# The first stage of a conv / mLSTM / MLA kernel: weights and input loaded by turns, two slabs in whole precision

## The chip, the cores and the metric

One core of a Trainium2 chip runs the whole program. The metric is the device time of one execution in microseconds. The kernel before took 2867.58 us (median of three runs, 2866.63 to 2867.74).

## The reference, cut to what matters

Two layers over 1024 latent and 256 context tokens of width 1024. Layer 0 mixes by a short convolution and an mLSTM, layer 1 by latent attention. Each layer begins with a modulation of its input, and only that of layer 0 is touched here:

```
sh_l, sc_l, g_l = split(silu(c) @ mod_w[0] + mod_b[0], 3)      # latent tokens
sh_c, sc_c, g_c = split(silu(c_ctx) @ mod_w[0] + mod_b[0], 3)  # context tokens
u_lat = x * (1 + sc_l) + sh_l
u_ctx = ctx * (1 + sc_c) + sh_c
gates = u @ ev_w_in[:, G0:G0+16]                               # 16 gate columns, in the same stage
```

All arithmetic is float32 in the reference.

## The kernel before, in words

`stage_modulate` is the first of the kernel's stages. It makes u transposed (features on the partitions, 1280 tokens along the rows) as a pair of tiles, `u_hi` and `u_lo`, whose sum is the float32 value: a high half in TensorE's rounded format (fp32r) and the rest. All large products of the kernel take three matmuls of such halves (`mm3`, L38 to L42: high x high, low x high, high x low).

The 1024 features go in eight blocks of 128, k = 0 to 7. A beat handles one block:

- A slab of `mod_w` is needed: columns 128k to 128k+127 of the shift and of the scale, for all 1024 input features, 8 x 256 float32 values on each partition. Slabs 0 and 1 are loaded alone, 2 and 3, 4 and 5, 6 and 7 as pairs (`load_slab`, L147). ScalarE copies a slab into its high half (`w_high`, L222), VectorE subtracts (`w_low`, L258).
- TensorE sums silu(c) times the slab into 4 rows (`row_sums`, L323): the four columns of `cs` (the high and low half of the two vectors) are the stationary side, and for each of the 8 blocks of input features the slab's high and low half move past, 16 matmuls of 256 columns. ScalarE copies the 4 rows out (L209).
- TensorE transposes the ten 128x128 tiles of the input (`turn`, L342), in three token chunks: j = 0 with 256 tokens (the context), j = 1 and 2 with 512 each, in the order 1, 2, 0.
- TensorE turns the 4 rows into columns with the matrix `sel` (`columns`, L332, the selection), and VectorE adds the bias (L267): now the scale and shift of block k stand one on each partition.
- ScalarE and VectorE evacuate the transposed tiles with that scale and shift: ScalarE writes `u_hi` for all three chunks (`high`) and the float32 value for chunk 2 (`whole`), VectorE the float32 value for chunks 0 and 1. Then VectorE subtracts for chunk 2 (`low`, L282), GpSimd for chunks 1 and 0 (L194).
- TensorE multiplies u by the gate weights (`gates`, L356), nine matmuls a block, two beats later.

The order on each engine is written out by hand, in one loop over k for each engine, with semaphores between them. TensorE: row sums of k, gates of k-2, transposes of k, selection of k; the gates of the last three blocks follow the loop. VectorE: column add, evacuations, `w_low(k + 2)`, `low(k, 2)`. ScalarE: `u(k)`, with the rows of k+1 copied inside it, then `w_high(k + 3)`.

All loads of the stage are issued by SyncE on one queue: c, ident, slab 0, `sel`, the bias, the input's block 0, slab 1, the gate weights, slabs 2 and 3, input blocks 1 and 2, slabs 4 and 5, input blocks 3 and 4, slabs 6 and 7, input blocks 5 to 7 (`SPANS`, L76), the gate bias, and the first weights of the next stage (L182), which ScalarE and VectorE also split here (L255, L318). The stage ends with a barrier of all engines.

Of the kernel before, what the change touches and what calls it, by code (L numbers as in the profile page):

```python
# [9 lines left out]
P = 128  # L10
KD = D // P
# [16 lines left out]
ALU = mybir.AluOpType  # L28
# [3 lines left out]
def f(ap):  # L32

    return ap.bitcast(F32)
# [39 lines left out]
def stage_modulate(nc, a, keep):  # L74

    SPANS = ((0, 1), (1, 3), (3, 5), (5, 8))  # L76
    PAIR_AT = (0, 1, 2, 0)
    u_hi, u_lo, mod_col, ident = keep["u_hi"], keep["u_lo"], keep["mod_col"], keep["ident"]
# [9 lines left out]
    with ExitStack() as ctx:  # L88
# [12 lines left out]
        cs = s.sb("cs", [P, KD, 4], F32R)  # L101
        sel = s.sb("sel", [4, 2])
# [6 lines left out]
        x_in = [[s.sem(f"x_in{q}{j}") for j in range(3)] for q in range(4)]  # L109
# [6 lines left out]
        u_hi_ok, u_raw_a, u_raw_d, u_lo_d, u_lo_p = (s.sem(n) for n in ("u_hi_ok", "u_raw_a", "u_raw_d", "u_lo_d", "u_lo_p"))  # L116
        gw_zero, gw_hi_ok, gw_ok, first_hi = (s.sem(n) for n in ("gw_zero", "gw_hi_ok", "gw_ok", "first_hi"))
# [24 lines left out]
        arrival = lambda k: k if k < 2 else 1 + k // 2  # L142

        @block.sync
        def _(sp):
# [51 lines left out]
        def _(act):  # L197
# [15 lines left out]
            def u(k):  # L213
                act.wait_ge(col_ok, k + 1)
                high(k, 1)
                high(k, 2)
                whole(k, 2)
                if 0 < k < KD - 1:
                    row_sums(k + 1)
                high(k, 0)  # L220

            def w_high(k):  # L222
                if k == 0:
                    for half in range(2):
                        act.wait_ge(w0_in[half], 16)
                        nc.scalar.copy(high_of(0)[:, :, half, :], slab(w_raw, 0)[:, :, half, :]).then_inc(w_hi_ok, 1)
                    return
                act.wait_ge(w_in[arrival(k)], 32)
                if k >= 2:
                    act.wait_ge(r_done, k - 1)  # L230
                nc.scalar.copy(high_of(k), slab(w_raw, k)).then_inc(w_hi_ok, 1)
# [5 lines left out]
            w_high(0)  # L237
            row_sums(0)
            w_high(1)
# [18 lines left out]
        def _(dve):  # L258
            def w_low(k):
                for half in range(2) if k == 0 else ():  # L260
                    dve.wait_ge(w_hi_ok, half + 1)
                    nc.vector.tensor_tensor(slab(w_lo, 0)[:, :, half, :], slab(w_raw, 0)[:, :, half, :], f(high_of(0)[:, :, half, :]), ALU.subtract).then_inc(w_lo_ok, 1)
                if k:
                    dve.wait_ge(w_hi_ok, k + 2)
                    nc.vector.tensor_tensor(slab(w_lo, k), slab(w_raw, k), f(high_of(k)), ALU.subtract).then_inc(w_lo_ok, 1)
# [16 lines left out]
            def low(k, j):  # L282
# [4 lines left out]
            nc.vector.memset(ones[:, :], 1.0).then_inc(ones_ok, 1)  # L287
            dve.wait_ge(c_t, 1)
# [3 lines left out]
                                    0.5, None, ALU.mult).then_inc(c_ok, 1)  # L292
            dve.wait_ge(cs_hi, 1)
            dve.wait_ge(c_ok, 1)
            nc.vector.tensor_tensor(cs[:, :, 2:4], c_silu[:, :, :], f(cs[:, :, 0:2]), ALU.subtract).then_inc(cs_ok, 1)
            w_low(0)
# [3 lines left out]
            for k in range(KD):  # L300
                columns(k)
                whole(k, 0)
                whole(k, 1)
                if k == 0:
                    w_low(1)
                    low(0, 2)
# [5 lines left out]
                else:  # L312
                    if k + 2 < KD:
                        w_low(k + 2)
                    low(k, 2)
                if k == KD - 2:
                    dve.wait_ge(first_hi, 1)
                    nc.vector.tensor_tensor(wv_lo[:, :, :], w_first[:, :, :], f(wv_hi[:, :, :]), ALU.subtract)  # L318

        @block.tensor  # L320
        def _(pe):
            def row_sums(k):
                pe.wait_ge(w_lo_ok, k + 2)  # L323
# [3 lines left out]
                for kk in range(KD):  # L327
                    nc.tensor.matmul(sums, cs[:, kk, :], high_of(k)[:, kk, :, :], start=kk == 0, stop=False)
                    last = nc.tensor.matmul(sums, cs[:, kk, :], slab(w_lo, k)[:, kk, :, :], start=False, stop=kk == KD - 1)
# [2289 lines left out]
```

## Time and profile before

| | us |
|---|---|
| median of the runs | 2867.58 |
| the profiled execution, its own time | 2864.85 |
| its span | 2863.1 |
| TensorE busy | 2829.3 (99%) |
| VectorE busy | 1543.3 (54%) |
| ScalarE busy | 1185.2 (41%) |
| GpSimd busy | 285.7 (10%) |

The page cuts the span into 40 slices of 71.6 us; the first slice is about the stage of this case:

```
PE   7999999999999999999999999999999999999998
PEld 5888888888888888888887888888888888888886
DVE  6646554555366536654353325666666666666544
ACT  6323322332233223342243315666666666666500
```

Each digit is the busy share of a slice in tenths. In the rows, PE is TensorE's matmuls, PEld its weight loads, DVE VectorE, ACT ScalarE, POOL GpSimd, SP SyncE. The granted clock is given as a share of 2.4 GHz, so 0.50 is 1.2 GHz.

### The profile page before, as it was taken

How to read it: one execution, taken by the hardware profiler on the slowest of the kernel's cores; microseconds unless marked ns; L12 is line 12 of the kernel's file. 1: busy time of each engine (PE TensorE's matmuls, PEld its weight loads, DVE VectorE, ACT ScalarE, POOL GpSimd, SP SyncE). 2: the span in 40 equal slices, each digit the busy share in tenths (PEclk: the TensorE clock that was granted, in tenths of full speed). 3: DMA queues.
4: the chain of work that ended last, by engine and by line, in shares of the span. 5: the costliest groups of instructions: out<-in, count | busy, mean ns of one | idle time of the engine just before them, and what ended most of it. 6: DMA issues, size and time to landing. Idle time of an engine off the chain costs nothing. (4 is left out here: it accounts for less than half of the span.)

```text
span 2863.1 us, 38077 instructions
## 1 busy us (share of the span) xinstructions
PE 2829.3 (99%) x15377; PEld 2430.1 (85%) x15377; DVE 1543.3 (54%) x2793; ACT 1185.2 (41%) x1979; POOL 285.7 (10%) x298
## 2 busy tenths in 40 slices
PE   7999999999999999999999999999999999999998
PEld 5888888888888888888887888888888888888886
DVE  6646554555366536654353325666666666666544
ACT  6323322332233223342243315666666666666500
POOL 5100000000000000001232001202202022020000
PEclk9999999999999999999999999999999999999999
DMA  7311130113111311163361320010000100002332
GB/s 211 100 34 47 47 122 26 53 49 114 32 47 47 116 39 48 45 217 103 111 196 51 126 81 34 27 35 23 28 26 27 38 20 32 26 24 103 126 102 75
DMA packets 221504, 200.76 MB, mean 70 GB/s; under 512 B 12085, under 2 KB 193221, under 8 KB 221330
## 3 DMA queue, kind: packets, MB, share of 16 engines
q1 hardware_dynamic: 208578, 184.91, 20.9%
q0 software_dynamic: 2352, 8.17, 0.8%
q10 hardware_dynamic: 10400, 5.24, 0.6%
q8 instruction: 123, 2.02, 0.3%
q14 instruction: 51, 0.42, 0.0%
HBM read 157.34 MB, written 40.95 MB: 69 GB/s over the span
## 5 line engine op out<-in xcount | busy, mean ns | idle before, releaser
L40 PE MATMUL e_pj<-e_u_hi,e_w_hi 128*128 128x512 f32 (+1 forms) x864 | 307.9, 356 | 1.0 <-PEq L58 1.0
L40 PE MATMUL e_pj<-e_u_hi,v_w_hi 128*128 128x512 f32 (+1 forms) x864 | 307.7, 356 | 0.2 <-DVE v_kk_lo L882 0.2
L41 PE MATMUL e_pj<-e_u_lo,e_w_hi 128*128 128x512 f32 (+1 forms) x864 | 306.0, 354 | 0.0
L41 PE MATMUL e_pj<-e_u_lo,v_w_hi 128*128 128x512 f32 (+1 forms) x864 | 306.0, 354 | 0.0
L42 PE MATMUL e_pj<-e_u_hi,v_w_lo 128*128 128x512 f32 (+1 forms) x864 | 305.8, 354 | 0.0
L42 PE MATMUL e_pj<-e_u_hi,e_w_lo 128*128 128x512 f32 (+1 forms) x864 | 305.7, 354 | 0.0
L2241 ACT CAST t_pt_hi<-t_ring 128x512 fp32r<-128x512 f32 (+1 forms) x384 | 181.4, 519 | 232.3 <-PE t_ring L2447 232.3
L2330 DVE TENSOR_TENSOR t_pt_lo<-t_ring,t_pt_hi 128x512 fp32r<-128x512 f32 (+1 forms) x384 | 216.0, 597 | 52.6 <-ACT t_pt_hi L2241 50.9
L2257 ACT ACTIVATE t_prob<-t_scores,t_bias 128x1280 f32<-128x1280 f32 x128 | 170.6, 1333 | 87.7 <-DVE t_bias L2351 87.5
L42 PEld LDWEIGHTS e_pj<-e_u_hi,v_w_lo 128*128 128x128 f32 x864 | 163.2, 189 | 23.2
L42 PEld LDWEIGHTS e_pj<-e_u_hi,e_w_lo 128*128 128x128 f32 x864 | 163.1, 189 | 23.1
L40 PEld LDWEIGHTS e_pj<-e_u_hi,v_w_hi 128*128 128x128 f32 x864 | 163.3, 189 | 22.4 <-issue 0.9
L40 PEld LDWEIGHTS e_pj<-e_u_hi,e_w_hi 128*128 128x128 f32 x864 | 163.2, 189 | 22.1 <-issue 1.2
L41 PEld LDWEIGHTS e_pj<-e_u_lo,v_w_hi 128*128 128x128 f32 x864 | 163.4, 189 | 20.7
L41 PEld LDWEIGHTS e_pj<-e_u_lo,e_w_hi 128*128 128x128 f32 x864 | 163.2, 189 | 20.4
L2262 ACT ACTIVATE t_prob<-t_prob,t_rec 128x1280 f32<-128x1280 f32 x128 | 177.0, 1382 | 7.4 <-DVE t_rec L2355 7.4
L2447 PEld LDWEIGHTS t_ring<-k_ident,t_prob 128*128 128x128 f32 x1280 | 147.2, 140 | 16.7
L2447 PE MATMUL t_ring<-k_ident,t_prob 128*128 128x128 f32 x1280 | 160.3, 272 | 0.0
L656 POOL TENSOR_TENSOR v_wgt<-v_wgt,v_mask 128x128 f32<-128x128 f32 x80 | 41.3, 519 | 1039.2 <-DMA v_wgt<-r_rows 1039.0
L40 PE MATMUL t_scores<-t_kn_hi,t_qn_hi 128*128 128x256 f32 x381 | 140.3, 368 | 2.0 <-ACT t_prob L2257 2.0
L41 PE MATMUL t_scores<-t_kn_lo,t_qn_hi 128*128 128x256 f32 x381 | 135.6, 356 | 0.0
L2500 PE MATMUL t_scores<-l_kr_lo,t_qs 128*128 128x256 f32 x381 | 135.6, 356 | 0.0
(500 smaller groups left out, 6700.2 us busy)
## 6 DMA issues: line engine op xcount, KB each, us to landing
e_w_raw<-in_ev_w_in SPq DMA_DIRECT2D x72, 512.0 KB, 4.7
v_mw<-in_mod_w SPq DMA_DIRECT2D x32, 512.0 KB, 3.7
l_w_raw<-in_od_w_in SPq DMA_DIRECT2D x21, 512.0 KB, 3.9
o_m_raw<-mixT SPq DMA_DIRECT2D x20, 512.0 KB, 5.4
o_w_raw<-in_ev_w_out SPq DMA_DIRECT2D x16, 512.0 KB, 8.8
zgT<-l_lat_q SPq DMA_DIRECT2D x16, 512.0 KB, 3.8
t_zg<-zgT SPq DMA_DIRECT2D x32, 256.0 KB, 2.8
ogT<-t_zg SPq DMA_DIRECT2D x32, 256.0 KB, 2.0
```

What stands on the lines that cost most here:

```text
L40: nc.tensor.matmul(out, whi, xhi, start=first, stop=False)
L41: nc.tensor.matmul(out, whi, xlo, start=False, stop=False)
L42: return nc.tensor.matmul(out, wlo, xhi, start=False, stop=last)
L656: pool.tensor_tensor(wgt[d][x][:, :], wgt[d][x][:, :], mask[:, d, :], ALU.add).then_inc(masked, 1)
L2241: nc.scalar.copy(dst, src).then_inc(ring_hi, 1)
L2257: nc.scalar.activation(prob[x][:, :], S[:, 0:T], ACT.Exp, bias=bias[x][:, :], accum_out=total[x][:, :]).then_inc(exp_ok, 1)
L2262: nc.scalar.mul(prob[x][:, :], prob[x][:, :], rec[x][:, :]).then_inc(prob_ok, 1)
L2330: nc.vector.tensor_tensor(dst, src, hi, ALU.subtract).then_inc(ring_free, frees(op))
L2447: last = nc.tensor.transpose(ps[:, c * P:(c + 1) * P], prob[t % 2][:, (c0 + c) * P:(c0 + c + 1) * P], ident[:, :])
L2500: last = nc.tensor.matmul(out, qs[b][:, tok], kr2[1][:, k0:k0 + n], start=False, stop=True)
```

## The change: what it does

- The input is loaded in five spans (0), (1), (2, 3), (4, 5), (6, 7), and the loads go by turns: input 0, slab 1, input 1, the gate weights, then for each pair its slabs and its input blocks.
- Slabs 0 and 1 are summed in whole precision: plain float32 matmuls of `c_rows`, a new tile of four columns (silu of the two vectors, and two columns of zero), with no halves made. Slab 0 goes by halves of 128 columns as they land.
- Of each slab from 2 on, the last two of the eight blocks of input features are also summed whole; only the first six are split (`split_blocks`), and the whole ones come first.
- The halves are made in other places: `w_high` and `w_low` of slabs 2 and 3 in beat 1; then `w_high(k + 2)` at the end of ScalarE's beat k, behind the copy of the rows, and `w_low(k + 1)` straight behind VectorE's column add.
- The copy of the rows moves from the middle of `u(k)` to behind it.
- TensorE's gates of k-2 move behind the selection, and two groups instead of three follow the loop.
- The split of the next stage's first weights moves one beat back on ScalarE (k = 6) and behind the loop on VectorE.

```diff
-    SPANS = ((0, 1), (1, 3), (3, 5), (5, 8))
+    SPANS = ((0, 1), (1, 2), (2, 4), (4, 6), (6, 8))
+    WHOLE, FIRST_SPLIT = 2, 2
+        split_blocks = slice(0, KD - WHOLE)
...
             load_x(0)
             load_slab(1, 1)
+            load_x(1)
             sp.dma_start(gw_raw[...], ...)
-            load_slab(2, 2)
-            load_x(1)
-            load_slab(4, 2)
-            load_x(2)
-            load_slab(6, 2)
-            load_x(3)
+            for q, k in enumerate((2, 4, 6)):
+                load_slab(k, 2)
+                load_x(2 + q)
...
             # ScalarE
-            w_high(0)
             row_sums(0)
-            w_high(1)
             u(0)
...
-            w_high(2)
             row_sums(1)
-            w_high(3)
             for k in range(1, KD):
                 u(k)
-                if k + 3 < KD:
-                    w_high(k + 3)
-                if k == KD - 3:
+                if k == 1:
+                    w_high(2)
+                    w_high(3)
+                if k + 1 < KD:
+                    row_sums(k + 1)
+                if 1 < k < KD - 2:
+                    w_high(k + 2)
+                if k == KD - 2:
                     act.wait_ge(first_in, 16)
                     nc.scalar.copy(wv_hi[:, :, :], w_first[:, :, :])
...
             # VectorE
             for k in range(KD):
                 columns(k)
+                if 3 <= k < KD - 1:
+                    w_low(k + 1)
                 whole(k, 0)
                 whole(k, 1)
+                low(k, 2)
...
+                if k == 1:
+                    w_low(2)
+                    w_low(3)
+            dve.wait_ge(first_hi, 1)
+            nc.vector.tensor_tensor(wv_lo[:, :, :], w_first[:, :, :], f(wv_hi[:, :, :]), ALU.subtract)
...
             # TensorE, row_sums(k)
+                if k == 0:
+                    for half in range(2):
+                        pe.wait_ge(w0_in[half], 16)
+                        for kk in range(KD):
+                            last = nc.tensor.matmul(sums[:, half, :], c_rows[:, kk, :], raw[:, kk, half, :], start=kk == 0, stop=kk == KD - 1)
+                elif k < FIRST_SPLIT:
+                    pe.wait_ge(w_in[arrival(k)], 32)
+                    for kk in range(KD):
+                        last = nc.tensor.matmul(sums, c_rows[:, kk, :], raw[:, kk, :, :], start=kk == 0, stop=kk == KD - 1)
+                else:
+                    pe.wait_ge(w_in[arrival(k)], 32)
+                    for kk in range(KD - WHOLE, KD):
+                        nc.tensor.matmul(sums, c_rows[:, kk, :], raw[:, kk, :, :], start=kk == KD - WHOLE, stop=False)
+                    pe.wait_ge(w_lo_ok, k - FIRST_SPLIT + 1)
+                    for kk in range(KD - WHOLE):
+                        nc.tensor.matmul(sums, cs[:, kk, :], high_of(k)[:, kk, :, :], start=False, stop=False)
+                        last = nc.tensor.matmul(sums, cs[:, kk, :], slab(w_lo, k)[:, kk, :, :], start=False, stop=kk == KD - WHOLE - 1)
...
             # TensorE, before and in the loop
+            pe.wait_ge(c_zero, 1)
+            pe.wait_ge(c_rows_ok, 1)
             pe.wait_ge(cs_ok, 1)
             pe.wait_ge(sel_in, 16)
             for k in range(KD):
                 row_sums(k)
-                if k == 2:
-                    pe.wait_ge(gw_ok, 4)
-                if 2 <= k < KD - 1:
-                    for j in ORDER:
-                        gates(k - 2, j)
                 for j in ORDER:
                     turn(k, j)
                 columns(k)
-            for k in (KD - 3, KD - 2, KD - 1):
+                if k == 2:
+                    pe.wait_ge(gw_ok, 4)
+                if k >= 2:
+                    for j in ORDER:
+                        gates(k - 2, j)
+            for k in (KD - 2, KD - 1):
                 for j in ORDER:
                     gates(k, j)
```

## Rows read from the trace of the kernel before

**Rows 1.** Windows: busy PE, PEld, DVE, ACT, POOL, then clock, DMA share, GB/s.

```profile
10.00:15.00 5.00, 4.84 (x23) 3.59 (x24) 0.09 (x2) 1.23 (x2) 0.00 (x0) 1.00 1.20 274
15.00:20.00 5.00, 1.40 (x9) 0.98 (x7) 3.12 (x4) 3.96 (x9) 1.53 (x1) 0.92 1.10 348
20.00:25.00 5.00, 4.35 (x21) 3.03 (x22) 5.00 (x7) 2.64 (x3) 2.87 (x2) 0.50 1.10 348
25.00:30.00 5.00, 5.00 (x33) 3.98 (x32) 3.21 (x5) 4.22 (x6) 1.18 (x1) 0.89 1.10 348
```

**Rows 2.** Timeline of TensorE, one beat: start us, busy us, engine, line, operation.

```profile
36.93 0.60 PE L337 MATMUL e_e<-m_sel,m_rows 4*128 4x2 f32 x4
37.46 0.28 PE L328 MATMUL e_z<-m_w_hi,m_cs 128*4 128x256 f32 x1
...
39.34 0.39 PE L40 MATMUL e_y<-e_u_hi,m_gw_hi 128*128 128x512 f32 x1
...
41.10 1.26 PE L353 MATMUL e_pj<-k_ident,m_x_tok 128*128 128x128 f32 x10
42.29 0.60 PE L337 MATMUL e_e<-m_sel,m_rows 4*128 4x2 f32 x4
```

**Rows 3.** Timeline of VectorE, one beat.

```profile
38.23 0.15 DVE L271 TENSOR_TENSOR k_mod_col<-e_e,k_b_col 128x4 f32<-128x4 f32 x1
...
39.30 0.81 DVE L280 TENSOR_SCALAR m_u_raw<-e_pj,k_mod_col 128x512 f32<-128x512 f32 x1 [0.27 <-ACT e_u_hi L203]
40.03 2.28 DVE L265 TENSOR_TENSOR m_w_lo<-m_w_raw,m_w_hi 128x2048 fp32r<-128x2048 f32 x1
42.23 1.77 DVE L285 TENSOR_TENSOR e_u_lo<-m_u_raw,e_u_hi 128x512 fp32r<-128x512 f32 x1
43.92 0.15 DVE L271 TENSOR_TENSOR k_mod_col<-e_e,k_b_col 128x4 f32<-128x4 f32 x1
```

**Rows 4.** Timeline of the start: column adds, slab 2's cast, second row sums.

```profile
16.50 0.16 DVE L271 TENSOR_TENSOR k_mod_col<-e_e,k_b_col 128x4 f32<-128x4 f32 x1 [6.41 <-PE e_e L337]
...
20.35 1.90 ACT L231 CAST m_w_hi<-m_w_raw 128x2048 fp32r<-128x2048 f32 x1 [0.63 <-DMA m_w_raw<-in_mod_w]
...
20.65 0.37 PE L328 MATMUL e_z<-m_w_hi,m_cs 128*4 128x256 f32 x1 [4.25 <-DVE m_w_lo L265]
...
24.02 2.25 PE L353 MATMUL e_pj<-k_ident,m_x_tok 128*128 128x128 f32 x10
...
26.84 0.17 DVE L271 TENSOR_TENSOR k_mod_col<-e_e,k_b_col 128x4 f32<-128x4 f32 x1 [1.42 <-PE e_e L337]
...
32.55 0.15 DVE L271 TENSOR_TENSOR k_mod_col<-e_e,k_b_col 128x4 f32<-128x4 f32 x1
```

**Rows 5.** Timeline of TensorE at 1005 us: plain float32 matmuls, two records each.

```profile
1005.77 1.02 PE L1142 MATMUL e_y<-v_acc,k_ones 128*2 128x512 f32 x2
1006.63 1.88 PE L1142 MATMUL e_z<-v_acc,k_ones 128*2 128x512 f32 x4
```

**Rows 6.** Groups by line and shape, 0 to 66 us: busy us, mean ns, idle before.

```profile
L262 DVE TENSOR_TENSOR m_w_lo<-m_w_raw,m_w_hi 128x1024 fp32r<-128x1024 f32 x2 | 2.5, 1225 | 3.2 <-ACT m_w_hi L226 3.2
```

**Rows 7.** Timeline of ScalarE, the same beat: its last evacuation of chunk 2.

```profile
39.75 0.78 ACT L207 ACTIVATE m_u_raw<-e_pj,k_mod_col 128x512 f32<-128x512 f32 x1
```

**Rows 8.** Timeline of the stage's end, on three engines.

```profile
60.68 0.15 DVE L271 TENSOR_TENSOR k_mod_col<-e_e,k_b_col 128x4 f32<-128x4 f32 x1
...
62.65 2.41 POOL L194 TENSOR_TENSOR e_u_lo<-m_u_raw,e_u_hi 128x512 fp32r<-128x512 f32 x2 [2.97 <-DVE m_u_raw L280]
...
63.02 1.44 DVE L285 TENSOR_TENSOR e_u_lo<-m_u_raw,e_u_hi 128x512 fp32r<-128x512 f32 x1 [0.46 <-ACT m_u_raw L207]
...
65.71 0.27 PE L42 MATMUL e_x<-e_u_hi,m_gw_lo 128*128 128x256 f32 x1
```

**Rows 9.** Issue of `sel` (timeline of SyncE), and the bias's landing (issues: KB, us).

```profile
3.04 0.72 SPq L165 DMA_DIRECT2D m_sel<-in_c_sel  x1
...
k_b_col<-in_mod_b_col SPq DMA_DIRECT2D x1, 16.0 KB, 4.1
```

More of the change, by code:

```diff
@@ L101, in stage_modulate @@
         cs = s.sb("cs", [P, KD, 4], F32R)
+        c_rows = s.sb("c_rows", [P, KD, 4])
         sel = s.sb("sel", [4, 2])
@@ L108, in stage_modulate @@
         gate_bank, r_bank = [x_bank[:, :], y_bank[:, :], z_bank[:, 0:512]], z_bank[:, 512:1024]
-        x_in = [[s.sem(f"x_in{q}{j}") for j in range(3)] for q in range(4)]
+        x_in = [[s.sem(f"x_in{q}{j}") for j in range(3)] for q in range(len(SPANS))]
         w_in = [s.sem(f"w_in{q}") for q in range(5)]
@@ L217, in u @@
                 whole(k, 2)
-                if 0 < k < KD - 1:
-                    row_sums(k + 1)
                 high(k, 0)
             def w_high(k):
[L223 to L227, printed above, removed]
                 act.wait_ge(w_in[arrival(k)], 32)
-                if k >= 2:
+                if k >= FIRST_SPLIT + 2:
                     act.wait_ge(r_done, k - 1)
-                nc.scalar.copy(high_of(k), slab(w_raw, k)).then_inc(w_hi_ok, 1)
+                nc.scalar.copy(high_of(k)[:, split_blocks], slab(w_raw, k)[:, split_blocks]).then_inc(w_hi_ok, 1)
             act.wait_ge(c_in, 32)
@@ L259, in w_low @@
             def w_low(k):
[L260 to L265, printed above, removed]
+                dve.wait_ge(w_hi_ok, k - FIRST_SPLIT + 1)
+                nc.vector.tensor_tensor(slab(w_lo, k)[:, split_blocks], slab(w_raw, k)[:, split_blocks], f(high_of(k)[:, split_blocks]),
+                                        ALU.subtract).then_inc(w_lo_ok, 1)
             def columns(k):
@@ L292, in _ @@
                                     0.5, None, ALU.mult).then_inc(c_ok, 1)
+            dve.wait_ge(c_ok, 1)
+            nc.vector.tensor_copy(c_rows[:, :, 0:2], c_silu[:, :, :]).then_inc(c_rows_ok, 1)
             dve.wait_ge(cs_hi, 1)
-            dve.wait_ge(c_ok, 1)
             nc.vector.tensor_tensor(cs[:, :, 2:4], c_silu[:, :, :], f(cs[:, :, 0:2]), ALU.subtract).then_inc(cs_ok, 1)
-            w_low(0)
             dve.wait_ge(b_in, 16)
@@ L301, in _ @@
                 columns(k)
+                if 3 <= k < KD - 1:
+                    w_low(k + 1)
                 whole(k, 0)
                 whole(k, 1)
+                low(k, 2)
                 if k == 0:
-                    w_low(1)
-                    low(0, 2)
                     for d in range(2):
@@ L310, in _ @@
                             nc.vector.tensor_tensor(split_cols(gw_lo, d, g), raw_cols(d, g), f(split_cols(gw_hi, d, g)), ALU.subtract).then_inc(gw_ok, 1)
+                if k == 1:
                     w_low(2)
[L312 to L318, printed above, removed]
+                    w_low(3)
+            dve.wait_ge(first_hi, 1)
+            nc.vector.tensor_tensor(wv_lo[:, :, :], w_first[:, :, :], f(wv_hi[:, :, :]), ALU.subtract)
         @block.tensor
@@ L322, in row_sums @@
             def row_sums(k):
-                pe.wait_ge(w_lo_ok, k + 2)
                 if k:
@@ L326, in row_sums @@
                 sums = r_bank[0:4, 0:2 * P].rearrange("r (h c) -> r h c", h=2)
-                for kk in range(KD):
-                    nc.tensor.matmul(sums, cs[:, kk, :], high_of(k)[:, kk, :, :], start=kk == 0, stop=False)
-                    last = nc.tensor.matmul(sums, cs[:, kk, :], slab(w_lo, k)[:, kk, :, :], start=False, stop=kk == KD - 1)
+                raw = slab(w_raw, k)
+                if k == 0:
[15 more added lines that the diff above has]
+                        last = nc.tensor.matmul(sums, cs[:, kk, :], slab(w_lo, k)[:, kk, :, :], start=False, stop=kk == KD - WHOLE - 1)
                 last.then_inc(r_done, 1)
```

2 lines of the change are left out of this document (added).

## The prediction

> **What bounds the kernel now.** I read the page first: TensorE is busy 99% of the span and only the first of the 40 slices has a 7 for it. So the kernel is bound by TensorE, and the first stage is one of the few places where it waits. Then I read the windows of the stage [rows 1]: 1.40 us busy between 15 and 20, 4.35 between 20 and 25, full after 25. The clock falls after the first pause (0.92 of the window, then 0.50) and comes back between 25 and 30. DMA is loaded throughout.
>
> Then the timeline, engine by engine. One beat of TensorE, from the selection of one slab to the next, is 36.93 to 42.29 = 5.36 us: selection 0.53 (to 37.46), 16 row-sum matmuls 1.88 (to 39.34, 0.1175 each), nine gate matmuls 1.76 (to 41.10), ten transposes 1.19 [rows 2]. One beat of VectorE is 38.23 to 43.92 = 5.69 us [rows 3]: column add, evacuations (the last ends at 40.11, 1.88 after the beat began), 2.28 for the low half of the weights, 1.77 for `low(k, 2)`. So in the middle VectorE sets the pace by 0.33 us a beat, and TensorE is nearly as long. At the start, the first column add comes at 16.50, the second at 26.84, the third at 32.55 [rows 4]. I measure everything from these adds (call them t0, t1, t2). From t2 to t7 at 60.68 [rows 8] is 28.13 us.
>
> **The steady beats, k = 2 to 7.** Six of eight blocks stay split: 12 x 0.1175 = 1.41 us. Two become one matmul each in whole precision. Its price is in the four records of `ones` against 512 columns: 1.88 us in all with its drain, two records each, and group starts 0.855 us apart [rows 5]; for 256 columns half, 0.43. So the row sums cost 1.41 + 0.86 = 2.27 instead of 1.88, and TensorE's beat is 5.36 + 0.39 = 5.75 us. The lowest price would be that of a split matmul (0.12 each: beat 5.13), the highest the 512-column price (0.855 each: beat 6.6). I take the middle, since the moving side has 256 columns.
>
> VectorE's `w_low` works on 1536 of 2048 columns: between 1.23 for 1024 [rows 6] and 2.28 for 2048 [rows 3], 1.75 us. ScalarE's cast, between three quarters of the 1.90 for 2048 columns [rows 4] and all of it, 1.47. VectorE's new beat: add 0.2, `w_low` 1.75, evacuations with their gaps 1.3, `low` 0.6 to 1.8: 3.9 to 5.1 us, below 5.75. (`low` takes 1.77 where it must wait for GpSimd's 512-column subtract; its own part is about 0.6.) ScalarE: 2.3 to the end of `whole` [rows 7], then 0.5, 0.35 and 1.47: 4.6 us. The moved `w_high` ends 1.8 us after the row sums it follows, TensorE's next selection 0.05 later: covered, barely; an overrun would cost only itself. The split halves are ready 1.95 us after the add, TensorE wants them 1.76 + 0.86 after it: covered. So the cadence passes from VectorE (5.69) to TensorE (5.75). Five beats: 28.75 against 28.13, a loss of 0.62 us. Putting the gates behind the selection changes the order within the beat, not its content.
>
> **The tail.** Three groups of gate matmuls follow the last selection, before and after. Before, the last of them ended at 65.98, 5.30 after t7; GpSimd's first subtract began 1.97 after t7, both together end at 65.06, and `low` at 64.46 [rows 8]. After, VectorE's add follows its selection at once, so TensorE has 3 x 1.76 ahead of it and ends about 5.4 after t7. The subtract of the first projection's weights is moved behind the last `low`: it is 1.23 for 1024 columns [rows 6] and starts when GpSimd is through, 4.38 after t7: 5.6. Tail: 5.6 instead of 5.3, a loss of 0.3. On that step the Trainium skill ("SBUF — State Buffer", Who interferes with whom) says that a VectorE operation with two SBUF inputs and a GpSimd operation that reads SBUF exclude each other for the whole instruction. The trace agrees, 1.77 beside 1.44 for the same `low` [rows 3, 8]; without the lock this step would cost 0.1, not 0.3. Net so far 0.62 + 0.3 = 0.9 lost. The gain is therefore (32.55 - t2) - 0.9, and all depends on the front.
>
> **The front.** Slab 0 is no longer cast nor subtracted; its sums start when half a slab and `sel` are there. `sel` is issued at 3.04, behind slab 0; `b_col`, issued at 3.80 just behind it, lands 4.1 us later, 7.9 [rows 9]. The wait for `sel`, until now hidden behind the casts, now decides: start 7.8. No row shows `sel` itself; were it two microseconds earlier, t2 would gain 1.1 at most, since the next slabs then set it. 16 whole matmuls of 128 columns cost 0.214 each at 2.4 GHz and 0.43 at 1.2 GHz. Ten transposes took 2.25 us at the low clock [rows 4], 1.19 at the high one [rows 2], so the engine starts low; it came back some 5.5 us after work resumed at 20.65 [rows 1, 4]. Hence 12.4 slow and 3.6 fast ones: end near 13.9. Transposes 1.2, selection 0.5, add: t0 = 15.6 against 16.50.
>
> Slab 1 has landed by then: 8 x 0.43 = 3.43, end 18.9; transposes (their block now a load of its own ahead of `gw`: 0.655 MB, landed near 16) and selection: t1 = 20.9 against 26.84. Six microseconds ahead, but slabs 2 and 3 now queue behind that block: 20.35 [rows 4] + 0.655 MB at some 300 GB/s [rows 1], 22.5. ScalarE finishes u(1) at 23.6 and then casts both slabs (25.1, 26.6); VectorE subtracts from 25.2 to 27.0; TensorE's 12 split matmuls start at 27.1. Between its selection at 20.8 and 27.1 TensorE has only 0.86 us of work (the whole blocks). t2 is then 27.1 + 1.41 + 1.19 + 0.53 + 0.15 = 30.4 at the high clock.
>
> But the present kernel lost the clock in a pause from 16.4 to 20.65 [rows 1, 4]. The new pause is 6.3 us with a burst in it. If it falls and comes back about 2.5 us after 27.1: sums 2.55, the rest fast, t2 = 31.5. If it stays low throughout, t2 = 32.5. The Trainium skill ("TensorE: Matmul & The Clock Gate", Part 1) says low is the default and only sustained activity lifts it; it speaks against this change, whose early lead is turned into idling. By that rule the middle case holds, without it the 30.4.
>
> Sum, forecast: t2 = 31.5, gain 1.05 - 0.9 = 0.15 us. Of the profiled run's 2864.85 (span 2863.1) this makes 2864.7; the median of the runs is 2.73 above it, so 2867.4.
>
> **Rivals.**
> 1. The clock stays up, or the start is earlier than `sel` lets me think: t2 = 30.4, gain 1.25, 2866.3 (29.5 at the best, 2865.4). For it: the burst of whole blocks in the pause. Against: the fall at 15 to 20 [rows 1].
> 2. Whole precision costs no more than a split matmul. Then TensorE's beat is 5.13, VectorE's about 5.2 leads, five beats take 26.0; slab 1's sums need 0.94, and the arrival of slabs 2 and 3 sets t2 = 29.0; end 29.0 + 26.0 + 5.6 = 60.6 against 65.98: gain 5.4, 2862.2. Against: 0.855 us spacing [rows 5].
> 3. The other side: the clock is low through slabs 0 and 1, whose sums are now all whole. Place: TensorE before t1. Price: sums 0 6.85 (end 14.6), transposes 2.15, selection, sums 1 6.85 again: t1 = 26.9, no lead left; ScalarE, VectorE and the split sums follow in series (u(1) 29.6, cast 31.1, subtract 33.0, sums 35.6, transposes and selection): t2 = 38.3, loss 5.8 + 0.9, 2874.3. It decides from the point where the clock is still low at about 16 us. Against: eight microseconds of unbroken work by then.
> 4. Slabs 2 and 3 land later than ScalarE is ready (23.6): each microsecond later moves t2 by one. Small-row loads ran at 274 GB/s, wide ones at 348 [rows 1]; two later: 2869.4. The change then does what it says, in order but not in time.
>
> **How the numbers follow.** Forecast 0.45, rival 1 0.33, rival 2 0.08, rival 3 0.04, rival 4 0.10. A measurement of this kernel can tell from no change about 0.2%, 5.7 us. Forecast, rivals 1 and 4 lie within it; rival 2 is at its edge (2861.9), and I give half of its chance and some unknown early gain to faster: 0.07; slower 0.04; same 0.89. The range takes in rivals 1 and 4 and most of 2, and half a microsecond of difference between sets of runs: 2862.5 to 2870.2. The forecast's own range, t2 from 30.8 to 32.5: 2866.7 to 2868.5.
>
> **What would show it.** TensorE's first row sum near 7.8; adds at 15.6, 20.9 and 31.5; the granted clock at half between about 23 and 29; row sums of 2.27 us and a beat of 5.75 us, VectorE idle in each; the stage's last instruction a VectorE subtract 5.6 after t7, near 65.8. I am wrong if the beat is under 5.4 us, if t2 is before 29 or after 33, or if the next stage starts more than 3 us from 67.0.

## The result, and the profile after

The changed kernel takes 2870.99 us (median of 20 runs, 2868.99 to 2873.22), the kernel before 2866.99 in the same session (20 runs, 2864.93 to 2870.07): ratio 1.0014, 95% interval [1.0008, 1.0020]. It is 4.0 us slower. That is inside the 0.2% named as the bound of no change, but outside the predicted range (2862.5 to 2870.2), and 3.6 us above the predicted 2867.4. The profiled execution of after took 2869.2 us, span 2867.4; that of before 2864.85, span 2863.1.

The first slice of the page still has a 7 for TensorE. TensorE is busy 2834.8 us instead of 2829.3.

**The front.** Timeline of TensorE in the changed kernel, from the start to the third selection (start us, busy us, engine, line, operation, in brackets the idle time before it and what ended it).

```profile
8.56 5.19 PE L323 MATMUL e_z<-m_w_raw,m_c_rows 128*4 128x128 f32 x32 [4.89 <-DMA m_sel<-in_c_sel]
...
15.46 3.62 PE L327 MATMUL e_z<-m_w_raw,m_c_rows 128*4 128x256 f32 x16
...
23.17 1.02 PE L331 MATMUL e_z<-m_w_raw,m_c_rows 128*4 128x256 f32 x4 [2.32 <-DMA m_w_raw<-in_mod_w]
26.93 0.38 PE L334 MATMUL e_z<-m_w_hi,m_cs 128*4 128x256 f32 x1 [2.74 <-DVE m_w_lo L257]
27.11 0.41 PE L335 MATMUL e_z<-m_w_lo,m_cs 128*4 128x256 f32 x1
...
29.45 2.33 PE L359 MATMUL e_pj<-k_ident,m_x_tok 128*128 128x128 f32 x10
31.72 0.83 PE L343 MATMUL e_e<-m_sel,m_rows 4*128 4x2 f32 x4
```

Windows of the same stretch, TensorE alone (busy, instructions, granted clock, DMA share, GB/s).

```profile
20.00:25.00 5.00, 1.88 (x11) 1.00 1.10 350
25.00:30.00 5.00, 3.07 (x15) 0.54 1.10 348
30.00:35.00 5.00, 5.00 (x25) 0.78 1.11 350
```

The first sums wait for `sel`, then two slabs pass without a stop, then TensorE does 0.86 us of whole blocks between 20.8 and 26.93. The split sums step by 0.21 us and the ten transposes take 2.33: half clock from shortly after 25 until about 32. One caution on the windows: they give 1.00 for everything ahead of the first recorded change, also where the matmuls run at the pace of half clock. In before, [rows 1] has 1.00 from 10 to 15 us, while the timeline steps by 0.21 us a matmul of 256 columns:

```profile
10.54 0.42 PE L328 MATMUL e_z<-m_w_hi,m_cs 128*4 128x256 f32 x1
10.75 0.42 PE L329 MATMUL e_z<-m_w_lo,m_cs 128*4 128x256 f32 x1
```

In after, TensorE starts 6 to 8 matmuls of 128 columns in each microsecond between 9 and 12, and 12 from 12 to 13: there the pace doubled, and the window again has 1.00 on both sides.

The column adds (VectorE):

```profile
15.64 0.16 DVE L264 TENSOR_TENSOR k_mod_col<-e_e,k_b_col 128x4 f32<-128x4 f32 x1 [6.87 <-PE e_e L343]
...
20.89 0.16 DVE L264 TENSOR_TENSOR k_mod_col<-e_e,k_b_col 128x4 f32<-128x4 f32 x1 [0.51 <-PE e_e L343]
...
32.59 0.16 DVE L264 TENSOR_TENSOR k_mod_col<-e_e,k_b_col 128x4 f32<-128x4 f32 x1 [4.04 <-PE e_e L343]
...
38.61 0.16 DVE L264 TENSOR_TENSOR k_mod_col<-e_e,k_b_col 128x4 f32<-128x4 f32 x1 [2.24 <-PE e_e L343]
...
62.62 0.16 DVE L264 TENSOR_TENSOR k_mod_col<-e_e,k_b_col 128x4 f32<-128x4 f32 x1 [2.35 <-PE e_e L343]
```

t1 is six microseconds ahead of before, t2 is level with it (32.59 against 32.55) [rows 4], t7 is 1.94 behind (62.62 against 60.68) [rows 8]. Before has a low stretch of the same length (19.2 to 26.1), so the clock alone doesn't make after the slower of the two; it takes back part of what the lead at t1 would have given.

**A beat.** TensorE again, one beat, from the gates behind one selection to those behind the next.

```profile
38.51 0.50 PE L40 MATMUL e_y<-e_u_hi,m_gw_hi 128*128 128x512 f32 x1
38.84 0.40 PE L41 MATMUL e_y<-e_u_lo,m_gw_hi 128*128 128x512 f32 x1
...
40.24 0.28 PE L42 MATMUL e_x<-e_u_hi,m_gw_lo 128*128 128x256 f32 x1
40.45 1.03 PE L331 MATMUL e_z<-m_w_raw,m_c_rows 128*4 128x256 f32 x4
41.41 0.28 PE L334 MATMUL e_z<-m_w_hi,m_cs 128*4 128x256 f32 x1
...
42.79 1.25 PE L359 MATMUL e_pj<-k_ident,m_x_tok 128*128 128x128 f32 x10
43.97 0.60 PE L343 MATMUL e_e<-m_sel,m_rows 4*128 4x2 f32 x4
44.50 0.50 PE L40 MATMUL e_y<-e_u_hi,m_gw_hi 128*128 128x512 f32 x1
```

38.51 to 44.50 is 5.99 us: gates 1.94, whole blocks 0.96, split sums 1.38, transposes 1.18, selection 0.53. VectorE is idle 2.3 us in each beat (the brackets of the adds), so TensorE sets the pace.

**The end.** The last gates end at 68.04 and the next stage begins at 69.19; before, it began at 67.02. So the stage itself costs 2.17 us in these two profiles. The spans differ by 4.3. The other 2.1 us lie behind the stage. Among TensorE's waits of after (in total, times, longest) is one that the first profile of before did not have, and one that was 0.2 us there:

```profile
PE e_pj L40 <- DVE o_w_lo L1269: 1.4, 1, 1.4
...
PE e_pj L40 <- DVE v_kk_lo L890: 0.7, 1, 0.7
```

### The profile page after: what moved, and what is told of

It is laid out like the page before. It is cut to its first block and busy times, and to the rows that moved or that the text cites. A ratio compares the mean times of both kernels' runs of the same rounds, so it can differ in the third digit from the quotient of the medians.

```text
span 2867.4 us, 38109 instructions
## 1 busy us (share of the span) xinstructions
PE 2834.8 (99%) x15393; PEld 2430.4 (85%) x15393; DVE 1532.2 (53%) x2792; ACT 1179.7 (41%) x1976; POOL 272.4 (9%) x298
## 5 line engine op out<-in xcount | busy, mean ns | idle before, releaser
L41 PEld LDWEIGHTS e_pj<-e_u_lo,v_w_hi 128*128 128x128 f32 x864 | 163.4, 189 | 20.8
```

Of the source, the lines that this page charges most:

```text
L41: nc.tensor.matmul(out, whi, xlo, start=False, stop=False)
```

## The experiments

Each run was compared with the kernel before on the same chip; "next stage" is the start of the second stage's first matmul in the profile. The medians of before were 2866.57, 2866.85 and 2867.01 in the three sessions (e0 to e3, e4 to e7, e8 to e11).

**e0: the changed kernel again, unchanged.**

> The changed kernel as it is, beside the kernel before on one chip. Its first profile ends the stage 2.2 us late (next stage at 69.19 instead of 67.02) and the whole span is 4.3 us longer; the other 2.1 us lie behind the stage (0.5 at the first head, 1.4 in a wait for an output weight's low half near 1275 us). Theory A: the stage's 2.2 us are the change's own and come again (column adds at 15.6, 20.9, 32.6, beats of 6.0 us), the 2.1 behind it are a transfer's chance and are different in another profile; time 2869 to 2872. Rival B: the change shifts the later stages into worse positions, and the same two waits come again with the same lengths.

2870.27 us, ratio 1.0009 [1.0000, 1.0018]; profiled 2868.02. Adds at 16.60, 21.84, 32.55, 38.54, 62.59, next stage 69.16; low clock from 24.2 to 31.1.

```profile
27.88 0.37 PE L334 MATMUL e_z<-m_w_hi,m_cs 128*4 128x256 f32 x1 [3.57 <-DVE m_w_lo L257]
...
30.40 1.58 PE L359 MATMUL e_pj<-k_ident,m_x_tok 128*128 128x128 f32 x10
31.91 0.60 PE L343 MATMUL e_e<-m_sel,m_rows 4*128 4x2 f32 x4
```

From t2 on the stage repeats within 0.1 us, but t2 is the same by two differences that cancel. Here t0 and t1 came 0.95 us later (the first sums took 6.35 us), so the split sums began at 27.88 instead of 26.93, and the clock was back earlier, so that the transposes took 1.51 us instead of 2.27. Theory A held for the stage. The wait for `o_w_lo` is there again (1.0), the one for `v_kk_lo` is not.

**e1: nothing whole after slab 1.**

```diff
-    WHOLE, FIRST_SPLIT = 2, 2
+    WHOLE, FIRST_SPLIT = 0, 2
```

> From slab 2 on all eight blocks are split again, slabs 0 and 1 stay in whole precision. Theory A (two whole blocks cost 0.96 us instead of 0.47, and going from float32 to fp32r matmuls and back costs about 0.1 us each time): TensorE's beat falls from 6.0 to about 5.45 us, VectorE has 2.28 instead of 1.75 in it and still idles; t2 is 33.0 to 33.5, since cast and subtraction of slab 2 grow by 0.4 and 0.5 and four more matmuls at the low clock by 0.9; stage end about 1.5 us earlier than in the changed kernel, 2868 to 2870. Rival: VectorE becomes the bound with the whole subtraction, beat 5.7 or more, and nothing is gained.

2873.8 us, ratio 1.0022 [1.0013, 1.0030], next stage 71.75. The beat is not shorter but longer, 6.67 us. Timeline of VectorE, ScalarE and TensorE in one beat of it:

```profile
50.45 1.90 ACT L226 CAST m_w_hi<-m_w_raw 128x2048 fp32r<-128x2048 f32 x1
...
52.38 2.29 DVE L257 TENSOR_TENSOR m_w_lo<-m_w_raw,m_w_hi 128x2048 fp32r<-128x2048 f32 x1 [0.41 <-ACT m_w_hi L226]
...
54.81 0.28 PE L334 MATMUL e_z<-m_w_hi,m_cs 128*4 128x256 f32 x1 [1.11 <-DVE m_w_lo L257]
...
56.85 0.36 ACT L213 COPY m_rows<-e_z 4x256 f32<-4x256 f32 x1 [1.07 <-PE e_z L335]
57.12 1.90 ACT L226 CAST m_w_hi<-m_w_raw 128x2048 fp32r<-128x2048 f32 x1
...
59.05 2.29 DVE L257 TENSOR_TENSOR m_w_lo<-m_w_raw,m_w_hi 128x2048 fp32r<-128x2048 f32 x1 [0.41 <-ACT m_w_hi L226]
```

No engine is full. One loop through all three sets the pace: sums, copy of the rows, cast of the next slab, subtract, sums: 0.16 + 0.27 + 1.93 + 2.43 + 1.88 (56.69 to 56.85, 57.12, 59.05, 61.48, and the sums) = 6.67. Theory A failed. The rival's number came true (a beat over 5.7 us, nothing gained), but not its cause, since VectorE idles in each beat. The whole blocks are dear on TensorE, but with the halves made only one beat ahead they are also what keeps this loop short (1.47 and 1.76 instead of 1.90 and 2.29, and 0.96 us of work that needs no halves).

**e2: the gates of k-2 back ahead of the transposes.**

```diff
                 row_sums(k)
+                if k == 2:
+                    pe.wait_ge(gw_ok, 4)
+                if k >= 2:
+                    for j in ORDER:
+                        gates(k - 2, j)
                 for j in ORDER:
                     turn(k, j)
                 columns(k)
-                if k == 2:
...
-                        gates(k - 2, j)
```

> The gates of k-2 stand between the row sums and the transposes again, as in the kernel before; the rest as changed. Theory A (the placing changes the order in a beat, not its content, but one switch between float32 and fp32r matmuls is saved): beat 5.9 instead of 6.0, t2 1.8 later, tail as long: the stage ends 1.0 to 1.4 us later, 2872. Rival (the gates behind the selection delay the next row sums and so the rows' copy, and that is where the beat's 0.25 us above the sum come from): beat 5.75, the stage ends no later.

2874.58 us, ratio 1.0026 [1.0017, 1.0035], next stage 73.08, adds 6.85 us apart. Both theories failed: they had beats of 5.9 and 5.75 us. TensorE in one beat:

```profile
52.75 1.03 PE L331 MATMUL e_z<-m_w_raw,m_c_rows 128*4 128x256 f32 x4
54.74 0.28 PE L334 MATMUL e_z<-m_w_hi,m_cs 128*4 128x256 f32 x1 [0.96 <-DVE m_w_lo L257]
...
56.12 0.40 PE L40 MATMUL e_y<-e_u_hi,m_gw_hi 128*128 128x512 f32 x1
...
57.88 1.25 PE L359 MATMUL e_pj<-k_ident,m_x_tok 128*128 128x128 f32 x10
```

That wait comes in every beat from k = 4 on: `w_low(k + 1)` stands behind the column add, and with only the whole blocks between the two it is not covered. From the whole blocks to the split sums it is 1.99 us, where in after, without a stop, it is 0.96: the wait costs 1.03 us a beat. The prediction's working had 1.95 us for the halves against 0.86 of whole blocks, so 1.1 without the gates. Without the wait the beat would be 6.85 - 1.03 = 5.82 us, 0.18 less than in after. The gates take 1.76 us here (56.12 to 57.88) and 1.94 in after, which is the same 0.18: the gates' new place covers 1.03 us and costs 0.18.

**e3: the pause filled.** Five float32 matmuls of 512 columns, whose result nothing uses, stand in it, two behind the gates' place of k = 1 and three behind the whole blocks of slab 2.

```diff
+            def fill(count):
+                for n in range(count):
+                    nc.tensor.matmul(y_bank[0:4, :]..., c_rows[:, 0, :], x_tok[:, 2:6, 0:P], start=True, stop=True)
...
+                    if k == 2:
+                        fill(3)
                     pe.wait_ge(w_lo_ok, k - FIRST_SPLIT + 1)
...
+                if k == 1:
+                    fill(2)
```

> Adds five plain float32 matmuls of 4x512 into a bank that is not yet in use, two behind the selection of block 1 and three behind the whole blocks of slab 2, so that TensorE is busy (some 4.3 us more) in the pause before slab 2's split sums. Theory A (the clock falls in that pause and stays low for the split sums and the transposes of block 2): the granted clock stays at 1.0, t2 at 30.4 to 30.7 instead of 32.6, the stage ends 2 us earlier than in the changed kernel, and the spread between its executions (2869 to 2873) gets smaller. Rival (the fillers delay the split sums by as much, or the clock falls anyway): t2 at 32.5 or later.

2867.68 us, ratio 1.0000 [0.9991, 1.0009]. The windows of the front, and of a later stretch:

```profile
20.00:25.00 5.00, 4.58 (x16) 1.00 1.10 349
25.00:30.00 5.00, 4.74 (x31) 1.00 1.10 350
30.00:35.00 5.00, 5.00 (x33) 1.00 1.10 348
120.00:126.00 6.00, 6.00 (x61) 0.87 0.02 7
126.00:132.00 6.00, 6.00 (x33) 0.56 0.34 90
```

The split sums begin at 26.73, almost as in after (26.93), but at full clock: t2 is 29.96 instead of 32.59, the beats are 6.02 as before, next stage 66.62. Theory A held. The run adds work only where TensorE stood idle, so what it changes is the clock. From the start of the split sums to t2 it takes 3.23 us, in after 5.66: the low clock costs 2.4 us there, and the other 0.2 of the 2.6 is the earlier start. Against e0 the same 2.6 at t2 are 1.4 of clock and 1.15 of start. The 2.6 us reach the end of the stage (69.19 or 69.16 to 66.62). The medians are 2.6 apart too (2870.27 and 2867.68), but each ratio is known only to 0.0009, which is 2.6 us. Firmer is the granted clock of all executions of the two: 0.9968 on average over the 11 of e0 and 0.9977 over the 11 here, which makes 18.3 and 13.0 us at half clock, 5.3 less, worth 2.6 us (an estimate: a microsecond at half clock loses half of itself). The run also shows the clock falling a second time, behind 124 us, with TensorE busy.

**e4 and e5: the gate columns spread.** Just ahead of that second fall stand five groups of ten 36x36 transposes (`gate_columns`). In e4 (the kernel before) and e5 (after) each group stands between two steps of the projection that follows, instead of all in a row.

```diff
                     last = mm3(nc, pj[j][:, 0:n], ...)
+                    if k < len(between):
+                        between[k]()
...
-                    gate_columns()
+                    between = [lambda q=q, x=x: gate_columns(q, x) for q, x in enumerate(("i", "f", "b", "m", "keep"))]
```

> The kernel before, with one thing changed in the second stage: the 50 small transposes of 36 columns (gate columns, five groups of 0.62 us, alone on TensorE for 3.1 us near 123 us) are spread between the eight steps of the projection that follows them. Theory A2: a second loss of the clock comes in that stretch in many executions (three of four experiment profiles have the granted clock at 0.5 from about 124 to 131 us, the first profiles of both kernels do not), each worth 3.4 us; spread, the stretch is never that empty, and the slower executions of the kernel before (2868 to 2870) vanish: median 2865.0 to 2865.8 instead of 2866.6. Rival B2: the spread of times has other causes (transfers), and median and range stay within 0.3 us.

> The changed kernel with the same spreading of the gate columns. Theory A2: the second loss of the clock goes here too; what is left against the kernel before with spreading is the first stage alone, 2.2 us and what its own clock costs in other executions: 2867.5 to 2869, range narrower than 2867.0 to 2872.4. The share of the 3.7 us between the medians that goes with the spreading is what the change cost through the second stretch. Rival B2: the median stays at 2870.

e4: 2870.18 us, ratio 1.0012 [1.0004, 1.0021]. The stage is as in before (next stage 66.67), yet the clock falls near 129 us and once more near 2631. e5: 2875.31 us, ratio 1.0030 [1.0018, 1.0042]. Spreading doesn't prevent the fall, and the time grows: by 3.3 us over before in e4, and by 4.8 more than e0's in e5, of which 1.7 lie in the stage. The theory that the unbroken row of small transposes brings the fall is wrong. e5 has one more use, since its first stage is that of after:

```profile
20.00:25.00 5.00, 2.59 (x10) 0.74 1.10 348
25.00:30.00 5.00, 3.20 (x16) 0.50 1.10 348
30.00:35.00 5.00, 5.00 (x18) 0.50 1.10 352
```

Here the clock was low already when the whole blocks of slab 2 ran (1.87 us instead of 1.02) and stayed low until 36.0: t3 at 40.17 instead of 38.6. The same code draws 6.8 or 13.7 us of low clock, and 0 or 1.7 us more of stage.

**e6: slab 2 whole too, one whole block in the rest, gates of k-1.** There is then no half to wait for in front of t2.

```diff
-    WHOLE, FIRST_SPLIT = 2, 2
+    WHOLE, FIRST_SPLIT = 1, 3
...
-                if k >= 2:
+                if k >= 1:
                     for j in ORDER:
-                        gates(k - 2, j)
+                        gates(k - 1, j)
-            for k in (KD - 2, KD - 1):
+            for k in (KD - 1,):
```

(`w_high(2)` and `w_low(2)` go, and the split of the first weights comes into the loop at k = 6.)

> From the changed kernel: slab 2 is summed whole too and one block instead of two of the slabs behind it; the gates of block k-1 instead of k-2 stand behind the selection, so those of block 0 fall in the pause; the first projection weights are split ahead of the last rows and inside the loop again. Theory A: TensorE sums slab 2 from its landing at 23.2 (3.6 us) instead of waiting for cast and subtraction until 26.9, the clock does not fall, t2 = 28.7, t3 = 34.5, beats of 5.8 us, t7 = 57.9, tail 4.8 instead of 5.5: the next stage starts at 63.8 instead of 69.2 (before: 67.0). Time 3 us under the kernel before if the second stretch behaves as there, up to 3.4 us more where the clock falls in it: 2863.5 to 2867. Rival: the chain rows' copy, cast, subtraction, split sums (0.36 + 1.68 + 2.1 + 1.65) comes to over 6 us a beat and t7 is past 59.

2867.79 us, ratio 1.0003 [0.9994, 1.0012]; clock 1.00 throughout the stage, adds at 28.69 and 34.48 as expected, then 41.33: slab 4 landed at 34.10, too late for its cast.

```profile
34.10 1.69 ACT L226 CAST m_w_hi<-m_w_raw 128x1792 fp32r<-128x1792 f32 x1 [0.88 <-DMA m_w_raw<-in_mod_w]
```

Next stage 65.79 instead of 63.8, and the time above the expected 2863.5 to 2867: 0.95 us by this wait, and in the tail the last gates wait 1.76 us for GpSimd. The beats, with one whole block, are 5.9 us.

**e7: the loads in the order and spans of before.**

```diff
-    SPANS = ((0, 1), (1, 2), (2, 4), (4, 6), (6, 8))
+    SPANS = ((0, 1), (1, 3), (3, 5), (5, 8))
...
-            load_x(1)
...
-                load_x(2 + q)
+                load_x(1 + q)
```

> The changed kernel with the spans and the order of the loads as before: slabs 2 and 3 ahead of input block 1. Theory A (the turns give t1 its lead, but t2 is set by slab 2's chain and the turns delay that slab by 2.3 us): t1 moves from 20.9 to about 25.5, since block 1 of the input lands near 24, and because ScalarE casts slab 2 only behind u(1), t2 moves by some 4 us to 36 or 37: time 2873 to 2875. Rival: slab 2 lands at 20.9 and t2 is no later than 33.

2873.5 us, ratio 1.0026 [1.0015, 1.0036], next stage 74.30. TensorE, timeline:

```profile
22.64 1.05 PE L358 MATMUL e_pj<-k_ident,m_x_tok 128*128 128x128 f32 x4 [3.38 <-DMA m_x_tok<-in_h]
...
32.71 0.38 PE L333 MATMUL e_z<-m_w_hi,m_cs 128*4 128x256 f32 x1 [4.27 <-DVE m_w_lo L256]
```

The transposes of block 1 wait for the input, t1 is 26.67 and t2 37.63, about as theory A had it. The loads by turns are worth 5 us of this stage. Part of the 5 us is clock: it was low from 22.8 to 36.4 in this profile.

**e8 and e11: the kernel before, two more profiles.**

> The kernel before, unchanged, for a second profile of it. The first profile of before was one of its faster executions (2864.85 us, the median of 45 runs is near 2866.9), and all later profiles of the after family show a wait of TensorE for the low half of the output weights (o_w_lo, 1.0 to 1.4 us, near 1275 us) that it did not have. Theory A (that wait, and a second fall of the clock near 125 to 135 us, belong to the executions and come to before as well): this profile shows at least one of the two, and its time is 2866 to 2868. Theory B (they come from the change, by the moment at which the first stage ends): this profile has neither, like the first, and lies within 1 us of 2864.9.

> The kernel before once more, unchanged, a third profile of it. Theory A: o_w_lo wait or second clock fall seen in at least one of the two further profiles. Theory B: in neither; next stage begins at 67.0 in all three.

2865.91 and 2865.93 us, spans 2864.1 both, next stage 67.67 and 67.22. No fall of the clock between 100 us and the tail in either, but e8 has one that neither other profile of before has, inside the stage: half clock from 59.5 to 63, behind a stop of 1.5 us. The wait for `o_w_lo` is there, but 0.3 and 0.4 us. In e11:

```profile
PE e_pj L40 <- DVE v_kk_lo L882: 0.4, 1, 0.4
PE e_pj L40 <- DVE o_w_lo L1261: 0.4, 1, 0.4
```

So before has those waits as well, at a third to a half of the length. Theory A held as it was worded, though not for the fall near 130 us. From the start of the second stage to the end it takes 2796.1, 2796.4 and 2796.9 us; after takes 2798.2 and 2797.0.

**e10: the stage of before ended later.** Twenty more transposes, whose output nothing uses, stand behind the last gates.

```diff
+            pe.wait_ge(u_raw_a, KD)
+            for n in range(20):
+                nc.tensor.transpose(tp_bank[1 + n // 10][:, P * (n % 4):P * (n % 4) + P], x_tok[:, n % 10, 0:P], ident[:, :])
```

> The kernel before with twenty more 128x128 transposes of the first input block behind the last gates of the first stage (their output is used by nothing): the whole stage as before, only its end 2.3 us later (20 x 0.119), so the next stage begins at 69.3, where that of after began (69.19). Theory A (what is lost in the stage is lost once, whatever stands behind it adds nothing of its own): median before + 2.3 = 2869.2, ratio 1.0008. Theory B (a later start of the second stage costs more than itself, by the waits and the clock behind it): before + 4, 2870.9 or more, ratio 1.0014, as for after.

2870.14 us, ratio 1.0014 [1.0005, 1.0023], next stage 68.83. The interval holds both theories' 2.3 and 4 us. What the profile adds is that the clock falls behind this later start too (TensorE, windows):

```profile
128.00:130.00 2.00, 2.00 (x18) 0.82 0.17 31
130.00:132.00 2.00, 2.00 (x11) 0.50 0.78 231
132.00:134.00 2.00, 2.00 (x18) 0.82 0.03 8
```

**e9: e6 with slab 4 loaded alone.** The experiments pointed here: the fastest front, and its one late landing mended.

```diff
-        arrival = lambda k: k if k < 2 else 1 + k // 2
+        arrival = lambda k: k if k < 2 else 5 if k == 5 else 1 + k // 2
...
+                if k == 4:
+                    load_slab(4, 1)
+                    load_slab(5, 1)
+                else:
+                    load_slab(k, 2)
```

> As the run with three slabs whole and one block whole in the others, but slab 4 loaded alone ahead of slab 5, not as one pair. There slab 4 landed at 34.1 and the add of block 4 came 6.85 us after that of block 3. Theory A (the pair's size holds slab 4 back): slab 4 lands near 31, the wait of 0.98 us before the split sums of block 4 goes, adds at 28.7, 34.5, 40.4, 46.3, 52.2, 58.5, next stage at 64.9, median 2867.0 (0.8 under that run). Rival B (rows of 512 bytes instead of 1 KB are slower to move, so the queue behind it is later by as much): slab 4 near 32.5, but slabs 6 and 7 or input blocks 4 and 5 late by 1 us, next stage within 0.3 of 65.8.

2866.11 us (2863.77 to 2868.32), ratio 0.9997 [0.9988, 1.0005]. Adds at 28.57, 34.39, 40.25, 46.12, 52.00, 58.29, next stage 64.66, all within 0.3 us of theory A. ScalarE:

```profile
33.03 1.68 ACT L230 CAST m_w_hi<-m_w_raw 128x1792 fp32r<-128x1792 f32 x1
```

The cast follows the copy of the rows and waits for no load. Rival B was right about the rate: a slab loaded alone has rows of 512 bytes instead of 1 KB, and the queue moved 304 GB/s from 25 to 30 us, against 348 in after. Nothing waited for it. This is the fastest version, 4 to 5 us under the changed kernel. Against the kernel before its stage is 2.6 us shorter, and its time can't be told from before's.

**All runs together.** Stage: start of the next stage, less the 67.3 that the three profiles of before give. Time: median, less before's median of the session. The stage is from one profile, the time from 6 to 20 runs. Of the three profiles of before, the latest start (67.67, e8) has the low stretch near 60 us in it.

| | stage | time | time less stage | clock low again near 130 us |
|---|---|---|---|---|
| after | +1.9 | +4.0 | 2.1 | no |
| e0 | +1.9 | +3.7 | 1.8 | no |
| e1 | +4.5 | +7.2 | 2.8 | yes |
| e2 | +5.8 | +8.0 | 2.2 | yes |
| e3 | -0.7 | +1.1 | 1.8 | yes |
| e4 | -0.6 | +3.3 | 4.0 | yes |
| e5 | +3.6 | +8.5 | 4.9 | yes |
| e6 | -1.5 | +0.9 | 2.5 | yes |
| e7 | +7.0 | +6.7 | -0.4 | no |
| e9 | -2.6 | -0.9 | 1.7 | yes |
| e10 | +1.5 | +3.1 | 1.6 | yes |

## Why the prediction was wrong

The forecast was no change (2867.4, a gain of 0.15 us); the loss was 4.0. By its own steps:

- **The start, t0 and t1: right in time, in t0 by luck.** The wait for `sel` decides, at 8.56 instead of 7.8, and t0 came at 15.64 (15.6) and t1 at 20.89 (20.9). The start was 0.76 us later than forecast, and the sums took 5.13 us (8.56 to 13.69) where I had reckoned 6.1: two misses that cancel. In the other eight profiles with these sums they take 4.9 to 6.4 us, depending on when the pace doubles, and t0 lies between 14.78 and 16.60.
- **t2, wrong by 1.1 us.** The instants were right (slab 2 at 23.17 for 22.5, split sums at 26.93 for 27.1). The step that failed is "if it falls and comes back about 2.5 us after 27.1". It fell and did not come back before the selection: 32.59, which is the 32.5 that I had worked out for a clock low throughout and had put at the edge of the forecast's own range. In after the clock was back 5.3 us after the split sums began, in e0 3.2, in e5 9.2; in e0 the rest of the delay came from the late t0. I had taken the middle case by the rule that the Trainium skill gives ("TensorE: Matmul & The Clock Gate", Part 1): low is the default, and only sustained activity lifts the clock. The trace agrees with it: behind a pause of 6.1 us with 0.86 us of matmuls, 2.5 us of split sums did not lift the clock. Rival 1, the clock staying up, would have given a t2 of 30.4; with the fill it was 29.96.
- **The beat, 6.00 instead of 5.75: wrong in size.** Five beats took 30.03 us, not 28.75: 1.3 us of loss beyond the 0.6 predicted. Of the 0.25 a beat, 0.18 is in the gates (1.94 for 1.76) and 0.07 in the sums (2.34 for 2.27). "Putting the gates behind the selection changes the order within the beat, not its content" is the sentence that failed. Two steps are longer in the new order: from the first to the second gate matmul behind the selection 0.33 us, which is 0.22 where the gates follow the split sums, and from the last gate matmul to the whole blocks 0.21, where it was 0.12 to the transposes. Together that is 0.20, of which the other gate steps give back 0.02. e2, with the old order and the same sums, has the gates at 1.76 again and puts the order at 0.18 a beat. The two whole blocks take 0.96, 0.48 each, for 0.43; the split sums take 1.38 for 1.41. That VectorE would no longer set the pace, and would idle in each beat, was right. That the split halves are covered by the gates was right too (e2).
- **The tail: right in the sum, not in its steps.** The last subtracts on VectorE and GpSimd:

```profile
64.59 2.44 POOL L196 TENSOR_TENSOR e_u_lo<-m_u_raw,e_u_hi 128x512 fp32r<-128x512 f32 x2 [2.49 <-DVE m_u_raw L273]
...
66.35 1.76 DVE L310 TENSOR_TENSOR e_w_lo<-e_w_raw,e_w_hi 128x1024 fp32r<-128x1024 f32 x1
```

VectorE's began 3.73 after t7 and not at 4.38, since its row starts beside GpSimd's and not behind it, and took 1.76 us instead of 1.23; the two misses cancel, and any wait for GpSimd lies inside the 1.76. In before the same subtract, also beside GpSimd's, took 1.75. The last subtract ended at 68.11, 5.49 after t7 (5.6); TensorE's last gates ended 5.42 after it (5.4). The next stage began 6.57 after t7 against 6.34 in before: a loss of 0.23 for 0.3.
- **Behind the stage: a term put at nothing.** The forecast carried the 2.73 us between profile and median over, as if nothing behind the stage could change. Of the 4.3 us between the first two spans 2.17 are the stage, 2.1 are behind it. Against three profiles of before and two of after the same split is 1.9 and 1.1. The table shows some 2 us between stage and time in nearly every variant. The 2.73 us themselves are in good part clock: the profiled execution of before was granted 0.9975 on average, 79 executions of before in the later sessions 0.9968, 4 us more at half clock, worth 2 us (an estimate).

The signs of error I had named did not fire: the beat was over 5.4, t2 lay between 29 and 33, and the next stage at 69.19 lay within 3 us of 67.0. They were drawn so wide that the stage could lose 2.2 us inside them. Rival 2 (whole precision as cheap as split) is ruled out by 0.48 against 0.12 us a matmul, rival 3 by t0 and t1, rival 4 by 23.17, ahead of ScalarE's 23.6.

What is shown: the low clock in the pause costs 2.4 us in after (e3, one edit, by its rows, and the granted clocks of its executions agree); the waits for `sel`, slab 2 and the halves by their rows; the cover by the gates and the 0.18 us a beat of their new place (e2), the price of a shorter lead in the loop of e1, and the loads by turns (e7). The two longer steps of the new order were read from rows; what makes them longer was not tried.

What stays open is the part behind the stage. Apart from e4, e5 and e7, a microsecond won in the stage is about one in the time, from e2 (+5.8, +8.0) to e9 (-2.6, -0.9). The offset of some 2 us between them and before is made, as far as the profiles show, of longer waits (0.7 and 1.4 instead of 0.2 to 0.4) and, in several profiles, of a second stretch of low clock. Spans from the next stage on are 2796.1 to 2798.2 us in the six profiles without it and 2798.8 to 2802.5 in the eight with it, or 2801.2 without e4 and e5, whose code differs there: it costs some 2 to 4 us where it comes. e10 has the code of before behind a later start and has it too, which speaks for a matter of timing and not of what was changed; e7, later still, has not. How often each kernel draws it can't be read from one profile each, but the granted clock is on record for nearly every execution, and a mean of 0.9968 is 18.3 us at half clock in all, 5.6 to 8.3 of them, by the profiles of the two kernels, at the very end of the program. The 79 executions of before average 18.3 us, its three profiles 14.2, 15.9 and 15.1. The 31 of after average 19.8, its two profiles 12.4 each. So executions of both kernels commonly have a low stretch that their profiles lack, before as well as after, which agrees with e10. Between the two kernels it is 1.5 us at half clock, worth about 0.7 of the 4 us (an estimate, and hardly above the scatter of the averages). By this estimate more than half of after's offset behind the stage is not clock. The longer waits are part of it; the rest, and why the second stretch comes, is not settled.

## What to carry to other kernels

A lead at the start is worth only what the next late thing leaves of it: six microseconds won at t1 were gone at t2, and the idle engine then paid for them in clock. Before a step is moved, ask what it covers and what it will stand next to: the gates' new place gave 1.03 us a beat in cover and took 0.18. A forecast time that comes true can hide steps that did not: t0 and the tail fitted because two errors cancelled. Where a change is worth a few microseconds of 2867, take more than one profile of the kernel before, and don't let the largest uncertain term (here the clock) sit in the middle of its bounds.

## What the hardware showed that I had not expected

- A whole float32 matmul with four stationary columns and 256 moving ones takes 0.44 to 0.48 us at full clock, a matmul of halves 0.117. Since halves need two (high and low), whole precision costs about twice as much and saves a cast and a subtract.
- The same matmul costs more by its neighbour: the first gate matmul took 0.33 us to the next behind the selection, 0.22 behind the split sums; float32 whole blocks began 0.21 us after the last gate matmul, float32 transposes 0.12 after it.
- The clock fell in a pause with work in it (0.86 us of matmuls in 6.1 us), and it fell at 124 to 134 us with TensorE busy in every window around it, during or just behind the last of 50 transposes of 36x36.
- For the same code the low stretch in the first stage was 6.8 us in two profiles and 13.7 in a third, and the pace of the first sums doubled 2.9 to 5.9 us after they began (an estimate from their lengths, 4.90 to 6.35 us, and the two steps, 0.214 and 0.107).
- `low(k, 2)` on VectorE takes 0.68 us when issued ahead of GpSimd's subtract, 1.44 to 1.77 when both want to run: with the new order the 0.68 comes in every beat but the first three and the last. GpSimd's two subtracts of a beat took 4.4 us in the middle beats of before and take 2.35 in those of after.
